# Gate and up products with the input as the stationary operand, a slot of its own for chunk 30, and two splits moved ahead of the last step

## The reference, cut to what matters

```python
h = silu(x @ w_in[:, :2816]) * (x @ w_in[:, 2816:])     # gate and up products
y = h @ w_out                                           # (2816, 1024), the down product
```

## Time and profile before

| | |
|---|---|
| time, median of 3 executions | 1999.14 us (1998.36 to 2000.56) |
| the profiled execution's own time | 1996.64 us |
| its span in the trace | 1994.8 us |
| PE busy | 1982.6 us, 99% of the span |
| DVE busy | 1270.3 us, 64% |
| ACT busy | 902.5 us, 45% |
| DMA | 358.31 MB, mean 180 GB/s |

### The profile page before, as it was taken

One profiled execution on the slowest core, in us unless ns is written; L12 is line 12 of the kernel. 1 busy time (PEld: TensorE's weight loads), 2 busy tenths in 40 slices (PEclk: granted clock), 3 DMA queues, 4 the chain that ended last, 5 costly groups with the idle time before them and its releaser, 6 DMA issues.

```text
span 1994.8 us, 31100 instructions
## 1 busy us (share of the span) xinstructions
PE 1982.6 (99%) x12424; PEld 1760.5 (88%) x12424; DVE 1270.3 (64%) x1272; ACT 902.5 (45%) x1017; POOL 273.2 (14%) x209
## 2 busy tenths in 40 slices
PE   8999999999999999999999999999999999999999
PEld 7999888889999999878889998888899989889998
DVE  6556698585557555798676556676755557666554
ACT  4444456444443444356543444454443445444442
POOL 0000651110000000562020000413100021230000
PEclk9999999999999999999999999999999999999999
DMA  8656444656555556444465554545555554565552
GB/s 276 199 180 196 139 149 136 211 172 208 188 192 190 190 183 194 167 143 153 148 232 180 189 190 148 178 153 200 178 196 182 193 176 139 174 211 171 188 193 102
DMA packets 249121, 358.31 MB, mean 180 GB/s; under 512 B 24640, under 2 KB 164544, under 8 KB 249024
## 3 DMA queue, kind: packets, MB, share of 16 engines
q1 hardware_dynamic: 248880, 356.85, 54.5%
q10 hardware_dynamic: 144, 0.10, 0.0%
HBM read 355.85 MB, written 1.05 MB: 179 GB/s over the span
## 4 chain that ended last, share of the span: by engine, by line
PE 95%; DVE 3%; DMA 1%; ACT 0%; issue 0%; SPq 0%; POOL 0%; DVEq 0%; ACTq 0%
PE bankA L421 18%; PE bankA L423 17%; PE bankA L422 17%; PE bankO L421 13%; PE bankO L422 12%; PE bankO L423 12%; DVE w_lo L415 1%; PE bankT L447 1%; PE bankT L1064 1%; DMA w_raw<-in_ffn_in_dram 1%; PE bankT L972 0%; PE bankO L1064 0%; PE bankO L953 0%; PE bankT L953 0%; PE bankO L972 0%; PE bankO L1048 0%
## 5 line engine op out<-in xcount | busy, mean ns | idle before, releaser
L415 DVE TENSOR_TENSOR w_lo<-w_raw,w_hi 128x2048 fp32r<-128x2048 f32 (+2 forms) x297 | 695.3, 2349 | 350.9 <-ACT w_hi L384 350.7
L384 ACT ACTIVATE w_hi<-w_raw 128x2048 fp32r<-128x2048 f32 (+2 forms) x297 | 563.3, 1901 | 416.6 <-PE bankA L423 293.4
L421 PE MATMUL bankA<-xT_hi,w_hi 128*128 128x256 f32 x1888 | 534.9, 283 | 0.0
L423 PE MATMUL bankA<-xT_hi,w_lo 128*128 128x256 f32 x1888 | 534.3, 283 | 0.0
L422 PE MATMUL bankA<-xT_lo,w_hi 128*128 128x256 f32 x1888 | 534.2, 283 | 0.0
L421 PEld LDWEIGHTS bankA<-xT_hi,w_hi 128*128 128x128 f32 x1888 | 362.2, 192 | 3.8 <-issue 1.3
L422 PEld LDWEIGHTS bankA<-xT_lo,w_hi 128*128 128x128 f32 x1888 | 362.1, 192 | 2.4
L423 PEld LDWEIGHTS bankA<-xT_hi,w_lo 128*128 128x128 f32 x1888 | 362.2, 192 | 0.0
L421 PE MATMUL bankO<-w_hi,xT_hi 128*128 128x512 f32 x432 | 176.1, 408 | 1.2 <-DVE w_lo L410 1.1
L422 PE MATMUL bankO<-w_lo,xT_hi 128*128 128x512 f32 x432 | 169.0, 391 | 0.0
L423 PE MATMUL bankO<-w_hi,xT_lo 128*128 128x512 f32 x432 | 168.9, 391 | 0.0
(11 more groups left out here) (374 smaller groups left out, 3046.0 us busy)
## 6 DMA issues: line engine op xcount, KB each, us to landing
w_raw<-in_w_in_dram SPq DMA_DIRECT2D x184, 512.0 KB, 4.5
w_raw<-in_ffn_in_dram SPq DMA_DIRECT2D x172, 512.0 KB, 4.7
w_raw<-in_ffn_out_dram SPq DMA_DIRECT2D x88, 512.0 KB, 4.2
w_raw<-in_w_ffn_in_dram SPq DMA_DIRECT2D x88, 512.0 KB, 4.7
w_raw<-in_w_ffn_out_dram SPq DMA_DIRECT2D x44, 512.0 KB, 4.2
w_raw<-in_w_out_dram SPq DMA_DIRECT2D x16, 512.0 KB, 4.5
w_raw<-in_w_o_dram SPq DMA_DIRECT2D x16, 512.0 KB, 4.5
w_raw<-in_w_br_b_dram SPq DMA_DIRECT2D x8, 512.0 KB, 4.5
```

Of the source, the lines that this page charges most:

```text
L384: act.activation(cut(W_HI[slot(ph, i)], n), cut(w_raw[:, i % RING, :], n), ACT.Copy).then_inc(hi_done, 1)
L415: dve.tensor_tensor(cut(W_LO[slot(ph, i)], n), cut(w_raw[:, i % RING, :], n), cut(W_HI[slot(ph, i)], n).bitcast(F32), ALU.subtract).then_i ...
L421: pe.matmul(dst, hi, whi, start=start, stop=False, skip_group_check=True)
L423: return pe.matmul(dst, lo, whi, start=False, stop=stop, skip_group_check=True)
```

## The change

In all six feed-forward phases:

- The gate and up products hold a 128x128 block of the input stationary and stream the weights. A chunk is 24 products of 512 columns, and bank A[tok] holds gates and ups of one half of the tokens (tok 0 or 1), tokens on the partitions.
- h therefore has to be transposed in every step, not only in the first: `h_transposes` puts four PE transposes of 128x128 ahead of the next gate and up products. For step 10 there are two pairs, one on each side of `down(31)` for half 0.
- tanh, the two DVE operations and, in step 10, the split of h are made for each half of the tokens (256 columns) instead of once for 512.
- Chunk 30 has a slot of its own ("own").
- On ACT and DVE chunk 30 is split ahead of step 9's tanh and h, chunk 31's high part between the two tanh of step 9, and both chunks of the next phase ahead of step 10's tanh and h.
- The tables of angles lie in `pT`, and some small buffers elsewhere.

```diff
-        OWN_SLOT = {"ffn": {0: EXTRA, 1: FIRST, 25: SPARE, 28: LATE, 30: SPARE},
+        OWN_SLOT = {"ffn": {0: EXTRA, 1: FIRST, 25: SPARE, 28: LATE, 30: OWN},
...
-            def gate_up(gg, i, between=None):
-                for h in range(2):
-                    if h == 1 and between:
-                        between()
-                    pe.wait_ge(lo_done, chunk_no(gg, i + h) + RING)
-                    for s in range(2):
-                        for q in range(2):
-                            for t in range(4):
-                                c = t * PANEL + s * 256 + q * P
-
-                                mm = three(pe, A[s][:, q * SEQ:(q + 1) * SEQ], W_HI[slot(ph, i + h)][:, c:c + P],
-                                           W_LO[slot(ph, i + h)][:, c:c + P], xT_hi[:, 4 * h + t, :],
-                                           xT_lo[:, 4 * h + t, :], h == 0 and q == 0 and t == 0, h == 1 and t == 3)
-                        if h == 1 and s == 0:
-                            mm.then_inc(gu_ready, 1)
+            def gate_up_half(gg, i, h):
+                pe.wait_ge(lo_done, chunk_no(gg, i + h) + RING)
+                for tok in range(TT):
+                    mm = pe_part(pe, slot(ph, i + h), A[tok], tok, 4 * h, 4, h == 0, h == 1, xT_hi, xT_lo)
+                    if h == 1 and tok == 0:
+                        mm.then_inc(gu_ready, 1)
...
+            def h_transposes(k, toks=range(TT), to=0):
+                for tok in toks:
+                    pe.wait_ge(h_ready, f * H_STEPS + (2 * k + tok + 1))
                     for t in range(2):
...
             with pe.Fori(1, FJ - 4) as j:
-
-                pe.wait_ge(h_ready, f * H_STEPS + (j + 2))
+                h_transposes(j)
                 gate_up(g + j, 2)
...
-            pe.wait_ge(hT_lo_done, f * FJ + (FJ - 1))
+            hT_made(FJ - 1)
+            h_transposes(FJ - 1, (0,))
             pe.wait_ge(lo_done, chunk_no(g, 31) + RING)
             down(31, 0, False, False, mid_hi, mid_lo)
-            pe.wait_ge(hT_lo_done, f * FJ + FJ)
+            h_transposes(FJ - 1, (1,), 1)
+            hT_made(FJ)
```

More of the change, by code:

```diff
@@ L648, in hT @@
-            def hT(k, dst, gg=None):
-                act.wait_ge(h_ready, f * H_STEPS + (k + 2))
-                if gg is not None:
-                    act.wait_ge(chunk_used, chunk_no(gg, 1) + RING)
-                act.activation(dst[:], h_sb[:].rearrange("p (t c) -> p t c", t=2), ACT.Copy).then_inc(hT_hi_done, 1)
-            first_tanh()
+            def hT(k, dst):
+                act.wait_ge(hT_psum, f * HT_STEPS + (k + 1))
+                act.activation(dst[:], T[0].rearrange("p (k c) -> p k c", k=2), ACT.Copy).then_inc(hT_hi_done, 1)
@@ L674, in act_ffn @@
             if before_last is not None:
                 before_last()
-            act_split(act, ph, g, 28)
-            act_split(act, ph, g, 29)
-            tanh(FJ - 2)
-            act_split(act, ph, g, 30)
+            for i in range(28, 31):
+                act_split(act, ph, g, i)
+            tanh(FJ - 2, A, g, 27, (0,))
+            act_split(act, ph, g, 31)
+            tanh(FJ - 2, A, g, 27, (1,))
+            act_split(act, ph, g, 32)
             hT(FJ - 2, mid_hi)
-            act_split(act, ph, g, 31)
@@ L699, in step @@
[L699 to L705 removed]
+            def step(k, banks):
+                for tok in range(TT):
+                    n = f * H_STEPS + (2 * k + tok + 1)
+                    c = slice(tok * 256, (tok + 1) * 256)
+                    dve.wait_ge(th_ready, n)
+                    dve.scalar_tensor_tensor(th_sb[:, c], th_sb[:, c], 1.0, banks[tok][:, 0:256], ALU.add,
+                                             ALU.mult).then_inc(t1_done, 1)
+                    dve.wait_ge(t1_done, n)
+                    dve.scalar_tensor_tensor(h_sb[:, c], th_sb[:, c], h_scale, banks[tok][:, 256:512], ALU.mult,
+                                             ALU.mult).then_inc(h_ready, 1)
@@ L709, in dve_ffn @@
             dve_split(dve, ph, g, 3)
-            for tok in range(TT):
-                c = slice(tok * 256, (tok + 1) * 256)
-                swiglu(f * H_STEPS + (tok + 1), th_sb[:, c], O[tok][:, 0:256], O[tok][:, 256:512], h_sb[:, c])
+            step(0, O)
             dve_split(dve, ph, g, 4)
-            dve.wait_ge(hT_hi_done, f * FJ + 1)
-            dve.tensor_tensor(hT_lo[:], T[0].rearrange("p (k c) -> p k c", k=2), hT_hi[:].bitcast(F32),
-                              ALU.subtract).then_inc(hT_lo_done, 1)
+            hT(0, hT_hi, hT_lo)
             dve_split(dve, ph, g, 5)
-            step(1, g, 3)
+            step(1, A)
             dve_split(dve, ph, g, 6)
@@ L730, in dve_ffn @@
             dve_split(dve, ph, g, 26)
-            step(FJ - 3, g, 24)
+            step(FJ - 3, A)
             if angles is not None:
```

166 lines of the change are left out of this document (85 added, 81 removed).

## The result

The changed kernel takes 1994.29 us (median of 9 executions, 1993.46 to 1995.63) against 1998.91 us for the kernel before on the same chip (9 executions, 1995.65 to 2000.56): ratio 0.998, 95% interval 0.9972 to 0.9989. It is 4.6 us faster. The forecast was 2001.0 us in a range from 1994.5 to 2008, no change. The profiled execution took 1995.63 us, with a span of 1993.8 us.

The account below looks back on a forecast made before the run. PE, busy 99% of the span, was taken to bound the kernel. Own work -9.0, small pieces -1.0, waits +1.0, +4.8, +4.2 and +2.0 summed to +2.0 us, giving 2001.1 us from the median; forecast 2001 us, range 1994.5 to 2008.

Parts of the forecast that it names:

- small pieces: Short waits at the start of next phases and slower first products behind 256-column ones go away: 1 us gained.
- The rule that spoke against the products: Gate and up products: a lone warm gap of N/2.4 + 2.5 ns leaves an estimated gain of 7 us.
- T: End of a feed-forward phase: the time when chunk 26's and 27's products end, put at D + 10.88.
- D: End of a feed-forward phase: the time when chunk 26's products start.
- step 9, the other five phases: PE waits for step 9's h behind chunk 31's split on ACT: 0.2 us, five times, 1.0 us.
- step 9, first phase: Tables also load in the first phase, chunk 31 lands 1.9 us later, and PE waits 2.0 us for h.
- step 10, three phases: Ahead of another feed-forward layer or second-kind mixer, PE waits 1.6 us before step 10's first transposes: 4.8 us.
- step 10, first and fourth phase: Ahead of a first-kind mixer, chunk 34 comes by six small DMAs, 6.5 us; wait 2.1 us, twice: 4.2 us.
- the third rival: ACT's split of chunk 31 precedes step 9's second tanh; a load of 6.5 us gives 2008 us; 30%.
- The splits arrive in time: Loads of chunks 31 and 34 take 4.8 and 5.2 us, waits 5 us or less, some 1994 us; 17%.
- The gain is eaten: PE does 9 to 10 us less but waits 10 to 14 us at steps 9 and 10: 1995 to 2003 us; 50%.
- The dearer products: Gate and up products of 512 columns cost as much as two of 256, 2038 us; 3%.

Follow-up runs that it names:

- Experiment 6: Changed kernel with chunk 34's splits moved back behind (DVE: behind step 10) and both tanh of step 9 ahead of chunk 31's split on ACT: 1987.45 us, ratio 0.9946.
- Experiments 3: Changed kernel with only chunk 34's splits moved back, on ACT between step 10's two tanh, on DVE behind step 10's h: 1989.12 us, ratio 0.9957.
- experiment 5: Changed kernel, unchanged, measured again in another group: 1995.42 us, ratio 0.9987 to the kernel before.
- experiment 2: Kernel before with only the change's order of splits on ACT and DVE, products as before: 2000.66 us, ratio 1.001.
- experiment 9: Changed kernel with both tanh of step 9 ahead of chunk 31's split on ACT, chunk 34's splits still ahead of step 10: 1996.37 us, ratio 0.9992.
- experiment 7: Changed kernel without three of four h transposes in steps 0 to 9 and one of two in each half of step 10: 1981.74 us, ratio 0.992.
- experiment 4: Changed kernel with chunk 30 back in the spare slot that chunk 25 has used: 1995.03 us, ratio 0.9986.
- experiments 11 and 12: Changed kernel, chunk 34's splits moved back, step 9's tanh both first, plus unused buffer of 64 or 32 bytes per partition: 1988.01 and 1988.92 us.

## Why the prediction was wrong

**Right: what bounds the kernel, and PE's own work.** The sum had -9.0 for products, transposes and the own slot, and -1.0 for small pieces. Experiment 6, which has all of PE's work and no wait, shows -10.5 us by its stretches, and 1987.5 us where the prediction wrote 1989 for no wait at all. By parts: a chunk from the ring 5.46 and 5.44 us (forecast 5.44), four transposes and their restart 0.35 + 0.11 us (0.47), the own slot 5.51 - 5.44 = 0.07 us a phase (0.16). A middle step takes 16.8 us, as forecast. The rule that spoke against the products (the Trainium skill, page "TensorE: Matmul & The Clock Gate", section "Back-to-back issue gap", which gives it for a lone product) fails here too: with the estimate of 7 us in place of 38.4, experiment 6 would have been some 20 us slower than the kernel before, and it was 10.8 faster.

**Right: where PE waits and for what.** Step 10 in the five phases with a next one, step 9 in the first, nothing in the loops, the clock full. Experiments 3 and 6 take the two causes away one by one.

**Wrong: the size of the waits.** The step that failed is the load of chunk 31: "other chunks are under way, so I take 5.4 us, with 4.8 and 6.5 as ends. Chunk 31 lands at T - 0.2". It took 591.80 to 596.57, 4.8 us, and landed at T - 1.0 (T = 597.56); in the other phases 4.8 to 5.1 us. Of the 0.8 us between T - 0.2 and T - 1.0 the load is 0.6; the rest is T itself, 11.02 us behind D and not 10.88, since the slower restart behind the transposes (0.11 us) was left out of T. Chunks 32 and 33 come right behind it and cost it little; they were themselves slowed (6.2 and 7.3 us). No run changed the load itself, so its size is read from these rows and not tested. All later links kept the forecast distances within 0.1 us: chunk 34 issued at T + 4.4 (forecast T + 5.2), 5.6 us to land (5.6), DVE free at T + 14.1 (T + 15.0). PE came at T + 14.1 (T + 14.3). So step 10 waits 0.8 to 1.2 us and not 1.6, and step 9 none and not 0.2.

| wait (us) | forecast | measured |
|---|---|---|
| step 9, the other five phases | 1.0 | 0 |
| step 9, first phase | 2.0 | 1.4 |
| step 10, three phases | 4.8 | 3.0 |
| step 10, first and fourth phase | 4.2 | 3.2 |
| sum | 12.0 | 7.7 |

(1.0, 0.8 and 1.2 us make the 3.0; 2.0 and 1.2 the 3.2.) The six small loads of chunk 34 took 6.3 us in the first phase (176.21 to 182.49) and 6.1 in the fourth, not 6.5. The difference of 4.3 us turns the forecast +2.0 into -2.3, and the stretches of the trace say -2.4. The measured 4.8 us lies at the lower end of the forecast's own bound, where the median of the earlier trace rows with the second DMA's 0.5 us, 4.7 us, would have put it. The load isn't the same in every execution: in experiment 5 one of them took 6.2 us, and that phase was 0.9 us longer than before, the longer chain of the third rival, once in six.

**Left open: the other 2.2 us.** -2.4 us is what the trace shows (-2.0 in experiment 5), and the two measurements gave -4.6 and -2.8 us. So of the 6.8 us between 2001.1 and 1994.3, 4.3 are waits, shown by rows, 0.2 are the kernel before (1998.91 us and not 1999.14), and some 2.2 us no trace here explains. One part of it may be spread: the same kernel's medians were 1997.13 and 1998.28 us before, 1994.29 and 1995.42 after. The profiled executions don't stand at a fixed distance from their medians either: 1996.64 us is 2.3 under the 1998.91 of its kernel, 1997.32 is 0.2 over its own set's 1997.13, and those of after are 1.3 over (1995.63) and 0.7 under (1994.76). The forecast took its 1998.6 from one execution and added 2.5 us for the median. The range's lower end, 1994.5, was drawn for waits of 5 us with no room for such spread.

**The rivals.** "The splits arrive in time" gave 1994 us for loads of 4.8 and 5.2 us; chunk 31's was 4.8, chunk 34's 5.2 to 5.6, and the case is half met: the waits became short but not under 5 us. That the measured 1994.29 us is its figure is partly luck, since the waits of 7.7 us account for 1996.7 (1999.14 - 2.4). "The gain is eaten" is what the mechanism shows (of 10 us, 7.7 eaten) at a smaller price. The dearer products did not occur, the longer chain only in the one phase of experiment 5.

## What to carry to other kernels

A faster main engine and a reordered helper engine must be costed together: the whole new order costs 2.8 us with the old products (stretches of experiment 2), and the two moves that experiment 6 takes back cost 8.0 us with the new ones, which need h 2.8 us earlier. The two figures are not of the same moves, so their difference is an indication. A transfer's splits belong behind the work that the bound engine waits for next: here a few moved lines turned a gain of 3 to 5 us into one of 10.7 (10.8 and 10.6 in two groups). Price a load by its own rows in the place where it stands, and give the range room for the spread of one execution on top of the terms.

## What the hardware showed that I had not expected

- A wait can be paid twice. In an idle time of 3.6 us (experiment 9), and within 1 us behind those of 2.4 and 2.1 us (experiment 7), the granted clock fell from 2.4 to 1.2 GHz (1.00 to 0.50). In experiment 9 the 12 products that followed took 5.07 us, with starts 427 ns apart, instead of 2.84 us. Behind the longest waits of the changed kernel, 1.84 us, and of experiment 4, 1.96 us, it stayed full.
- Equal products have unequal spacing by the place of the slot that they stream from: 227 ns from ring and late (5.44 / 24), 230 from spare and own (5.51 / 24) in the changed kernel, 233 from spare before and 233 to 234 in experiments 11 and 12, all at full clock.
- Four transposes slow the first product behind them: 0.31 us to the next start (600.64 to 600.95) instead of 0.23; one transpose does the same (452.94 to 453.26 in experiment 7).
